# Two layers in one launch: rows of 2048 bytes for two activation tiles, and the sliding-window q projection in two TensorE passes a block

## The reference

```python
def swa_mixer(h, positions, w_in, sinks):
    proj = h @ w_in
    q, k, v, gate = jnp.split(
        proj, [SWA_WIDTH, SWA_WIDTH + SWA_KV_WIDTH, SWA_WIDTH + 2 * SWA_KV_WIDTH], axis=-1)
    q = rope(q.reshape(B, S, SWA_Q_HEADS, SWA_HEAD_DIM), positions, SWA_ROPE_DIM)
    k = rope(k.reshape(B, S, SWA_KV_HEADS, SWA_HEAD_DIM), positions, SWA_ROPE_DIM)
    y = swa_sink_attention(q, k, v, sinks)
    return y, gate
...
    x = x + (y * jax.nn.silu(gate)) @ w_out
```

## Time and profile before

| What | Value |
|---|---|
| median of 3 runs | 2737.94 us |
| the profiled execution | 2738.0 us |
| its span, first to last instruction | 2736.2 us |
| PE busy | 2703.8 us (99%) |
| DVE, ACT, POOL busy | 2031.5, 1451.9, 310.3 us |
| mean granted TensorE clock | 0.998 of full speed |
| DMA | 472.69 MB, mean 173 GB/s |

### The profile page before, as it was taken

How to read it: one execution, slowest core, us unless ns; L and a number is a source line. 1 busy time by engine, 2 the same in 40 slices (tenths; PEclk the granted TensorE clock), 3 DMA queues, 4 the chain that set the end, 5 groups by cost and what they waited for, 6 DMA issues and landing times.

```text
span 2736.2 us, 50882 instructions
## 1 busy us (share of the span) xinstructions
PE 2703.8 (99%) x17549; PEld 2448.1 (89%) x17549; DVE 2031.5 (74%) x3698; ACT 1451.9 (53%) x2565; POOL 310.3 (11%) x323
## 2 busy tenths in 40 slices
PE   7999999999999999999999999999999999999998
PEld 6999999999998888888888888888888998888887
DVE  7888888888888566667765665756777677788876
ACT  6566556655665444444453444534545665466663
POOL 0000000000000000004700000000370001500024
PEclk9999999999999999999999999999999999999999
DMA  6444444444444555566565555555555455554445
GB/s 223 145 158 142 156 148 154 151 150 155 147 149 135 182 188 187 185 193 221 179 193 191 183 191 184 188 195 184 195 174 191 162 167 164 185 169 147 152 158 182
DMA packets 130238, 472.69 MB, mean 173 GB/s; under 512 B 15136, under 2 KB 15136, under 8 KB 129952
## 3 DMA queue, kind: packets, MB, share of 16 engines
q1 hardware_dynamic: 126144, 457.37, 51.4%
q0 software_dynamic: 3936, 13.28, 1.5%
HBM read 468.33 MB, written 2.25 MB: 172 GB/s over the span
## 4 chain that ended last, share of the span: by engine, by line
PE 96%; DVE 2%; ACT 1%; issue 1%; DMA 0%; DVEq 0%; SPq 0%; ACTq 0%
PE bank L312 41%; PE bank L313 21%; PE bank L314 8%; PE bank L316 8%; PE bank L315 8%; PE bank L897 1%; PE bank L852 1%; PE bank L906 1%; DVE w_lo L288 1%; PE bank L1121 1%; PE bank L1269 1%; PE bank L964 0%; PE bank L1192 0%; ACT w_hi L282 0%; PE bank L1285 0%
## 5 line engine op out<-in xcount | busy, mean ns | idle before, releaser
L288 DVE TENSOR_TENSOR w_lo<-raw,w_hi 128x1024 fp32r<-128x1024 f32 x862 | 1058.4, 1253 | 164.8 <-ACT w_hi L282 160.8
L282 ACT ACTIVATE w_hi<-raw 128x1024 fp32r<-128x1024 f32 x862 | 896.7, 1053 | 424.6 <-PE bank L313 416.1
L312 PE MATMUL bank<-ya,w_hi 128*128 128x512 f32 x1792 | 625.7, 393 | 0.7 <-DVE h L2265 0.7
L312 PE MATMUL bank<-ux,w_hi 128*128 128x512 f32 x1744 | 619.0, 397 | 0.1
L313 PE MATMUL bank<-ya,w_lo 128*128 128x256 f32 x1792 | 501.0, 280 | 0.0
L313 PE MATMUL bank<-ux,w_lo 128*128 128x256 f32 x1744 | 487.5, 280 | 0.0
L314 PE MATMUL bank<-u,w_hi 128*128 128x272 f32 (+1 forms) x1296 | 407.9, 315 | 6.1 <-DVE u L439 4.2
L312 PEld LDWEIGHTS bank<-ya,w_hi 128*128 128x128 f32 x1792 | 336.5, 188 | 77.6 <-issue 2.2
L312 PEld LDWEIGHTS bank<-ux,w_hi 128*128 128x128 f32 x1744 | 327.6, 188 | 74.4 <-issue 2.9
L316 PE MATMUL bank<-u,w_lo 128*128 128x272 f32 (+1 forms) x1296 | 373.3, 288 | 0.0
L315 PE MATMUL bank<-u,w_hi 128*128 128x272 f32 (+1 forms) x1296 | 372.4, 287 | 0.0
(11 more groups left out here) (421 smaller groups left out, 3839.6 us busy)
## 6 DMA issues: line engine op xcount, KB each, us to landing
raw<-in_stream SPq DMA_DIRECT2D x864, 512.0 KB, 3.4
mix_row<-rows POOLq DMA_DIRECT2D x16, 408.0 KB, 5.1
xT<-in_xT SPq DMA_DIRECT2D x4, 544.0 KB, 5.8
mix_coef_m<-meta_rows POOLq DMA_DIRECT2D x16, 128.0 KB, 3.6
h<-in_xT POOLq DMA_DIRECT2D x1, 2048.0 KB, 9.7
out_dram<-h SPq DMA_DIRECT2D x8, 256.0 KB, 2.4
consts<-in_consts POOLq DMA_DIRECT2D x1, 1753.0 KB, 8.9
meta_rows<-mix_b_mat POOLq DMA_DIRECT2D x16, 1.0 KB, 3.3
```

The source lines that it names most:

```text
L282: act.activation(w_hi[:, slot], raw[:, slot], ACT.Copy).then_inc(hi_ready, 1)
L288: dve.tensor_tensor(w_lo[:, slot], raw[:, slot], w_hi[:, slot].bitcast(F32), ALU.subtract).then_inc(lo_ready, 1)
L312: pe.matmul(o, a, x, start=first, stop=False)
```

## The change

`BLOCK` becomes 512 words, so that the rows of `ux` and `ya` lie 2048 bytes apart; what is placed behind `ya` in SBUF moves down by 1536 bytes. The q tiles of the sliding stage get the whole bank as output, and with it the form of one 512-column and one 256-column pass a block. A new step `q` on VectorE, at block 17, adds the halves of the bank into `q_s` and releases the PSUM buffer. ACT's step, now `turn q` at block 18, waits for this release and makes `q_turned` by the same four copies, out of `q_s` instead of the bank; ACT's own copy to `q_s` goes. `rope` moves from 22 to 23 in VectorE's list.

```diff
-BLOCK = 2 * SEQ + 24
+BLOCK = 2 * SEQ
...
-            (17, "evac q"), (19, "values"), (33, "tanh"), (40, "exp", 0), (42, "exp", 1), (53, "p t", 0),
+            (18, "turn q"), (19, "values"), (33, "tanh"), (40, "exp", 0), (42, "exp", 1), (53, "p t", 0),
...
-            (22, "rope"), (33, "gate v"), (34, "maxima", 0), (36, "maxima", 1), (36, "gate"), (45, "scale", 0),
+            (17, "q"), (23, "rope"), (33, "gate v"), (34, "maxima", 0), (36, "maxima", 1), (36, "gate"), (45, "scale", 0),
...
-                    o = proj[b][:, :] if x else proj[b][:, 0:SEQ]
+                    o = proj[b][:, :]
...
-            def swa_evac_q(n):
-                await_slab(act, "swa", 4 * n - 3)
-                if n > 2:
-                    act.wait_ge(sem("head s"), HEADS + 2 * n - 4)
-                b, _ = tile_no("swa", 2 * n - 2)
-                turned_half(proj[b][:, 0:SEQ], SWA_Q_TURNS + n - 1)
-                act.activation(q_s[:, n % 2], proj[b][:, 0:SEQ], ACT.Copy).then_inc(tile_free[b], 1)
+            def swa_turn_q(n):
+                await_tile(act, "swa", 2 * n - 2)
+                turned_half(q_s[:, n % 2], SWA_Q_TURNS + n - 1)
...
+            def swa_q(n):
+                await_slab(dve, "swa", 4 * n - 3)
+                if n > 2:
+                    dve.wait_ge(sem("head s"), HEADS + 2 * n - 4)
+                b, _ = tile_no("swa", 2 * n - 2)
+                sum_halves(q_s[:, n % 2], b).then_inc(tile_free[b], 1)
+
```

More of the change, by code:

```diff
@@ L1790, in swa_y_hi @@
                     sem("swa hi"), 1)
-            steps_act = {"evac q": swa_evac_q, "values": swa_values, "tanh": swa_tanh, "exp": swa_exp,
+            steps_act = {"turn q": swa_turn_q, "values": swa_values, "tanh": swa_tanh, "exp": swa_exp,
                          "p t": lambda n, s: turned_out(HEADS + 2 * n - 1 + s, s), "y hi": swa_y_hi}
@@ L2514, in swa_y_lo @@
                                   ALU.subtract).then_inc(sem("swa lo"), 1)
-            steps_dve = {"rope": swa_rope, "gate v": swa_gate_v,
+            steps_dve = {"q": swa_q, "rope": swa_rope, "gate v": swa_gate_v,
                          "gate": swa_gate, "maxima": swa_maxima, "scale": swa_scale, "y": swa_y, "y lo": swa_y_lo}
```

## The result

| | before | after |
|---|---|---|
| median | 2737.97 us (6 runs, 2737.03 to 2738.28) | 2758.97 us (6 runs, 2757.78 to 2759.59) |
| the profiled execution | 2738.0 us | 2759.59 us, span 2757.7 |
| up to the first score step | 2423.09 us of the span | 2420.32 |
| first to last score step, 15 turns | 209.82 us | 233.82 |
| behind the last score step | 103.30 us | 103.56 |

A forecast was written before the change was run, and what follows sets the result against it. PE was taken to bound the kernel (96% of the span), VectorE having about 1 us spare per sliding turn. 2738.0 - 2.6 (rows) + 21.8 (hand-over) = 2757.2 us, range 2750 to 2761.

The forecast's parts named there:

- the overlap with the upper row gain: Lower end of the range, given as 2750 us: ACT's copies overlapping (16.4 us lost) with a row gain of 6.6 us.
- Rows of 2048 bytes: Wide blocks of line 312 on `ux` and `ya`: 346.7 instead of 347.5 ns, 3280 blocks, 2.6 us gained on PE.
- Two passes for three: Sliding stage's 256 q blocks: 8 ns less each, 2.0 us, counted as nothing because PE would not bound the stage.
- The hand-over: Sliding stage, q sum from VectorE to ACT and back: both work in turn, 1.45 us more a turn, 21.8 us lost.
- the loop: One sliding turn replayed from gate sum to gate sum through VectorE and ACT: 15.44 us against 13.99.
- The first stall: PE's first wait at the values of the sliding stage, after 1.8 us of spare is used up: 0.8 us.
- The end: After the last sliding turn, at the transposes: about as much lost again as the first turn lacked.
- It all fits: Rival: the new step fits the engines' spare, PE keeps the pace, 4.6 us gained, 2733.4 us; chance 0.05.
- The copies overlap: Rival: ACT's four copies from SBUF overlap, 1.36 us, loss 16.4 us, 2751.8 us; chance 0.2.
- Row length does nothing: Rival: no gain from rows of `ux` and `ya`, loss as forecast, 2759.8 us; chance 0.12.
- The clock falls: Rival: PE's stalls of 1.5 us in every 15 halve its clock in the sliding stage, 2860 us; chance 0.02.

The follow-up runs named there:

- base_96: `rows_only` with the placed activation tiles 64 bytes higher in SBUF (cursor + 96 instead of + 32); 2750.86 us.
- base_224: `rows_only` with the placed activation tiles 192 bytes higher in SBUF (cursor + 224 instead of + 32); 2758.01 us.
- rows_only: The kernel before with only BLOCK changed, to 2 * SEQ (rows of 2048 bytes); 2732.73 us, ratio 0.9983.
- sum_first: The changed kernel with VectorE's q sum at block 16, ahead of the second head's scaling and the slab split; 2732.04 us, ratio 0.9981.
- spare_sum: Kernel before with 2048-byte rows and two passes, ACT reading q from the bank's left half, VectorE summing an idle bank into an unread tile; 2731.12 us, ratio 0.9978.

## Why the prediction was right

- **Direction and size.** 2757.2 was forecast, 2758.97 measured, inside the range. Against its own profiled execution the forecast was 2738.0 - 2.6 + 21.8; measured were - 2.77, + 24.0 and + 0.26. The lower end of the range does not come out of its own terms: the overlap with the upper row gain is 2738.0 - 6.6 + 16.4 = 2747.8 and not 2750.
- **Rows of 2048 bytes** were right in the gain: 202 blocks of `ya` in 70.03 us, as named, and 2.77 us up to the first score (0.14 of it is the first q tile, 16 blocks by 8.5 ns). The reason was not right: the length does not decide. `base_96` and `base_224` have the same length and are 18 and 25 us slower than `rows_only`, far more than this gain. That the rows of the changed kernel came to lie where a block takes 346.67 ns was luck; nothing in the prediction looked at the address.
- **Two passes for three** were rightly counted at nothing here, but the 2.0 us that they would bring if PE bound the stage was wrong in size: some 3 of the 8 ns, 0.8 us, as `rows_only` showed. The turns of `rows_only` and `sum_first`, 13.87 and 13.83, agree: 15 x 0.04 = 0.6.
- **The hand-over** was the right mechanism, with the waits that it named: ACT 2.7 us (2.8 forecast), VectorE 1.85 (1.8), PE 1.7 (1.4, which left out that PE's own turn fell to 13.83); all steps of the loop are off by 0.04 us or less but one, the first copy of the probabilities, which took 0.52 and not 0.38. The four copies took 1.76, between the 1.72 chosen and the upper bound of 1.80. Together 0.14 us a turn were missed, 2.1 in 15 turns.
- **The first stall** was mis-sized: 0.8 was forecast, 1.71 came. The forecast started the first turn with VectorE as far ahead as in the kernel before. But VectorE is late already: in the q tile ahead of the first scores the sum, the four copies and the rotary operations stand one behind the other, with nothing beside them, and the gate sum comes 0.70 us after the first scores (2421.02 against 2420.32). Before the change it came 0.06 ahead of them (2423.03 against 2423.09). The next q sum therefore starts 9.40 us behind the scores (2429.72), and not the 8.83 at which the rotary operations stood before (2571.79, scores at 2562.96): 0.57 of the 0.9 that were missed. The rest is the steps of the loop that took longer (0.04 and 0.14) and 0.14 from the end of the second copy to the values.
- **The end.** The sum is 15 times 1.45 only if the 0.65 us that the first turn lacks are lost behind the last score step. There the transposes of the probabilities wait for VectorE's scaling, which ends at 2660.15, and PE stands 0.48 us in front of them (2660.26); less the 0.2 that its 256 blocks on `ya` gain, the part is 0.26 longer. The place was right, the size somewhat less.
- **The rivals.** "It all fits" fell for this order and is true of `sum_first`, which is 4.8 us under its kernel before; the 4.6 named are close by luck, since most of the 2.0 in them for the passes belongs to where the rows lie; VectorE's microsecond of spare was enough for the work, as `spare_sum` shows, and not for the wait. "The copies overlap" fell: four copies in 1.73 us end to end. "Row length does nothing" fell in its number, 346.7 ns came, though the length is indeed not what decides. "The clock falls" fell: the granted clock was 1.00 in this stage with PE standing still 1.7 us in every 15.6.

The Trainium skill, TensorE: Matmul & The Clock Gate, Part 1, gives the start-to-start distance of passes by their columns alone; by it the pair would take an estimated 325 ns in every one of these kernels. The traces do not agree: the means are 346.65 to 353.31 ns. The page says nothing of the pace by address; the prediction's "whatever the address" reads its formula, which has the columns alone.

## What to carry to other kernels

An engine's spare time does not tell what a new operation on it costs where another engine waits for the result: replay the loop from one release to the next in the order in which each engine works its list. Put the operation that hands over as early as its data is there, so that work which needs nothing from the other engine lies behind it; here two places further up in one list were worth 27 us. And when buffers are moved or padded, look at the step of the matmuls before and after: a shift of 192 bytes alone was worth nearly as much, 25 us.

## What was not expected of the hardware

- The pace of a wide and a narrow pass changes with where the activation tiles lie: 346.67, 347.5, 350.0, 351.67 and 353.31 ns a block, in repeating patterns of 1, 2, 3, 4 or 8 blocks, steady over hundreds of blocks. The same rows can run at two paces in two stages of one run (`base_224`: 353.31 and 346.67).
- On ACT the copies of 32 partitions do not overlap, from SBUF either: 1.73 us for four, while the operations of full height in the same rows start before the one ahead has ended. Behind such copies out of SBUF the next two operations do not overlap either: the copy of the probabilities takes 0.49 us and the split starts 0.52 after it, where before the same pair started 0.38 apart and the second pair after the change 0.37. This is the 0.14 us of the loop; its cause was not tried, and the full-height copy that stood between the four and this pair before the change (line 1768) is gone as well.
